# Last unit of the expert gather: eight late second halves and five homed rows instead of five and three

## The chip, the cores and the metric

One core of a Trainium2 chip runs the whole program. The metric is the device time of one execution in microseconds (us), lower is better; the figure for the kernel before is the median of three runs.

## What is computed

One decoder layer on 512 tokens of width 1024, all in float32: a mixing layer (stick-breaking attention beside a gated MLP), then an expert retrieval layer ("PEER"), then an input embedding gated by a sigmoid, with a layer norm after each. The change lies where the retrieval ends and the gate of the last 128 tokens begins:

```python
def block(args):                       # one tile of 128 tokens, 8 heads, 16 picks each
    xb, idb, gb = args
    ue = jnp.take(u_tab, idb, axis=0)
    h = jnp.einsum('thkd,td->thk', ue, xb)
    act = gb * jax.nn.gelu(h, approximate=False)
    ve = jnp.take(v_tab, idb, axis=0)
    return jnp.einsum('thk,thkd->td', act, ve)
...
x = layer_norm(ALPHA * x + ffn, ln2_g, ln2_b)
gate = jax.nn.sigmoid(x @ ple_wgate + ple_bgate)
x = layer_norm(ALPHA * x + gate * (p @ ple_wproj), ln3_g, ln3_b)
```

## The kernel before

The retrieval is cut into 32 units (NU), a unit being one head of one tile of 128 tokens; a unit has 16 picks (TOPK), which are called rows here. For each row GpSimd issues an indirect DMA (`gather_unit`, L658) that brings, for each of the 128 tokens, the 1024 numbers of the expert's u and, behind them in memory, the 1024 of its v: 8 KB to a partition, 1 MB in all. VectorE multiplies u by the token's x and sums it (`dots`, L1819), ScalarE takes the gelu and the gate and scales v by it (`activate`, L1435, L1438, L1445), and TensorE adds v, transposed in eight 128x128 blocks, to two banks of PSUM (`combine`, L1187). Consecutive units of one tile form a run; at a run's end VectorE adds its sum to the accumulator `acc` of the tile.

The rows lie in a ring of 13 parts of 1024 columns. A row takes two neighbouring parts, its u part being free again after five rows (U_LIFE) and its v part after eight (V_LIFE). So the issue of row n waits for the dots of row n-5 and for the combine of row n-8, both counted over all units. The issues stand in GpSimd's program in the order of the rows, and all of them go through one DMA queue.

The last unit, number 31, is treated differently:

- Rows from HOMED on (13, 14 and 15) go to buffers outside the ring, to `v_flat`, `wq_a` and `wq_r`, and wait only for the last query product, which was done long before.
- Rows from LATE on (11 to 15) are loaded without the last 512 columns of v ("late second halves"). Rows 14 and 15 are loaded as u alone at first, and the first half of their v follows in gathers of its own (L666).
- The late second halves come last on GpSimd, in gathers of 128x512 (L672, 0.25 MB each).
- For rows with a late half, ScalarE scales 512 columns instead of 1024, and `combine` does four block transposes instead of eight. The second halves are scaled and summed on VectorE into `late_sum` (`add_late`: L1889 for the first, L1892 for each further one), and their sum is turned into the PSUM bank by four transposes at once (L844).

Behind the last row VectorE's program has this order: scaling of row 15 (L2045), the addition of the upper PSUM half (`add_half`, L1880), of the lower one (`add_head`, L1873 and L1875), all `add_late`, then the upper half of y (L2055), its statistics (L1550 to L1561), a second `add_half` (L1880), centring and scaling (L1573, L2064, L1928), and the arguments of the gate (`gate_args`, L1918) that read TensorE's products. TensorE's program has the transposes of the accumulator (L844), the first half of the gate product of the columns 0 to 288, transposes, the first half of the columns 288 to 576, then a wait for the last `add_late`, the transposes of `late_sum`, two more first halves, and `second_half(0)` to `second_half(3)` (L1082, all in float32; each matmul leaves two records). SyncE waits for the last late gather before it stores the other three tiles' results.

The order around the change is written by hand, with semaphores; there is no planner.

Of the kernel before, what the change touches and what calls it, by code (L numbers as in the profile page):

```python
# [15 lines left out]
P = 128  # L16
D = 1024
S = 512
NT = S // P
# [5 lines left out]
PH, TOPK, NKEY = 8, 16, 128  # L25
# [16 lines left out]
HALF = D // 2  # L42
REST = S - P

LATE = TOPK - 5
HOMED = TOPK - 3
GV_RING = 5
# [137 lines left out]
def build(nc, a, out):  # L185
    ctx = ExitStack()
    with ctx:
# [76 lines left out]
        def row(u, c):  # L264

            if u == NU - 1 and c >= HOMED:
                return (v_flat, wq_a, wq_r)[c - HOMED]
            part = (FIRST_PART + U_LIFE * (u * TOPK + c)) % PARTS
            return ring[:, part * D:(part + 2) * D]

        late_sum = row(NU - 1, LATE)[:, PART:2 * D]
# [183 lines left out]
        picks_ready = sem("picks_ready")  # L455
        mean_spread = sem("mean_spread")
        bias_spread = sem("bias_spread")
        bias_kept = sem("bias_kept")
        gate_arg = sem("gate_arg")
        gain_in = sem("gain_in")  # L460
        ln2_in = sem("ln2_in")
        ln3_in = sem("ln3_in")
        proj_in = sem("proj_in")
        gain_spread = sem("gain_spread")
# [13 lines left out]
        def _(sp):  # L478
# [100 lines left out]
            for p in (piece_of(NT - 1, 5), piece_of(NT - 1, 6)):  # L579
                sp.wait_ge(piece_taken[p % 2], p // 2 + 1)  # L580
            sp.dma_start(b_gate[0:1, :], a["ple_bgate"][:, :]).then_inc(gain_in, 16)
            for i, name in enumerate(("ln2_g", "ln2_b")):
                sp.dma_start(gain_rows[i * KD:(i + 1) * KD, :], a[name][0, :].rearrange("(k n) -> k n", k=KD))\
                    .then_inc(gain_in, 16)
            for dst, src in ((w_gate, a["w_gate"][:, :, :]), (pT, a["pT"][:, :, :])):
                sp.dma_start(dst, src).then_inc(tail_in, 16)
            sp.wait_ge(q_done, Q_NO[17] + 1)
            for dst, name in ((ln2_g, "ln2_g"), (ln2_b, "ln2_b")):
                sp.dma_start(dst[0:1, :], a[name][:, :]).then_inc(ln2_in, 16)
            load_wq(23)  # L590
            sp.wait_ge(sums_done, 2)
            sp.wait_ge(q_done, Q_NO[29] + 1)
            for k in range(2):
                sp.dma_start(w_proj[k], a["w_proj"][:, k, :]).then_inc(proj_in, 16)
            load_wq(21)
            sp.wait_ge(q_done, Q_NO[30] + 1)
            sp.wait_ge(gate_done, 2)
            for dst, name in ((ln3_g, "ln3_g"), (ln3_b, "ln3_b")):
                sp.dma_start(dst[0:1, :], a[name][:, :]).then_inc(ln3_in, 16)
            load_wq(26)  # L600
# [9 lines left out]
        def _(pool):  # L610
# [25 lines left out]
            def gather_unit(u):  # L636
                if u:
                    pool.wait_ge(ids_ready, u + 3)
                for c in range(TOPK):
                    if u == 0 and c in (0, 1, TOPK // 2):  # L640
                        pool.wait_ge(ids_ready, (0, 1, TOPK // 2).index(c) + 1)
                    if u == 0 and c == 0:
                        pool.wait_ge(score_done, 1)
                    if u == 0 and c == 4:
                        pool.wait_ge(gv_halves, 1)
                    if u == 0 and c == 7:
                        pool.wait_ge(gv_halves, 2)
                    if u == NU - 1 and c >= HOMED:
                        pool.wait_ge(q_done, NU)
                    else:  # L650
                        if u * TOPK + c >= U_LIFE:
                            pool.wait_ge(dots_done, u * TOPK + c - U_LIFE + 1)
                        if u * TOPK + c >= V_LIFE:
                            pool.wait_ge(slot_free, u * TOPK + c - V_LIFE + 1)
                    n = PART if u == NU - 1 and c >= LATE else 2 * D
                    if u == NU - 1 and c >= TOPK - 2:
                        n = D
                    nc.gpsimd.indirect_dma_start(  # L658
                        out=row(u, c)[:, 0:n], out_offset=None, in_=a["uv"][:, :],
                        in_offset=bass.IndirectOffsetOnAxis(ap=ids[:, u % 4, c:c + 1], axis=0),  # L660
                    ).then_inc(rows_in[c % V_LIFE], 16)
# [15 lines left out]

        @block.tensor
        def _(pe):
# [355 lines left out]
            def spread_gain(n):  # L1035
                if n == 0:
                    pe.wait_ge(ln2_in, 16 * 2)
                    pe.wait_ge(cols_kept, 1)
                elif n == 4:
                    pe.wait_ge(ln3_in, 16 * 2)  # L1040
                    pe.wait_ge(gate_arg, 2)
                else:
                    pe.wait_ge(gain_kept, n)
                mm(ps[:, 6 if n < 4 else 4, :], neg_one[0:1, :], gains[n // 2][0:1, n % 2 * HALF:(n % 2 + 1) * HALF],
                   start=True, stop=True).then_inc(gain_spread, 1)

            def gain_columns():

                pe.wait_ge(gain_in, 16 * 3)
                nc.tensor.transpose(ps[:, 6, 0:2 * KD], gain_rows, ident[0:2 * KD, 0:2 * KD]).then_inc(cols_done, 1)  # L1050
# [36 lines left out]
            def spread_mean():  # L1087

                pe.wait_ge(sums_kept, 1)
                pe.wait_ge(picks_ready, 2)  # L1090
                for j in range(2):
                    k = mm(ps[:, 4 + j, :], picks[:, 0, :], sum_rows[:, j * HALF:(j + 1) * HALF], start=True, stop=True)
                k.then_inc(mean_spread, 1)

            def spread_bias(j):

                if j:
                    pe.wait_ge(bias_kept, 1)
                else:
                    pe.wait_ge(gain_kept, 4)  # L1100
                mm(ps[:, 6, :], picks[:, 1, :], sum_rows[:, j * HALF:(j + 1) * HALF], start=True, stop=True)\
                    .then_inc(bias_spread, 1)

            def embedding_product(i, j, bank):
                t = TAILS[i]
                if i == 0 and j == 0:
                    pe.wait_ge(proj_in, 16 * 2)
# [66 lines left out]
            def combine(u, c):  # L1174
# [9 lines left out]
                for k in range(KD // 2 if halved else KD):  # L1184
                    if very_last and k == 0:
                        pe.wait_ge(last_scaled, 1)
                    i = mm(ps[:, run_bank(r) + k // 4, (k % 4) * P:(k % 4 + 1) * P],  # L1187
                           row(u, c)[:, D + k * P:D + (k + 1) * P], ident[:, :], is_transpose=True,
                           start=(first and k % 4 == 0), stop=last or (u == NU - 1 and c == LATE - 1 and k >= 4),
# [68 lines left out]
        def _(act):  # L1258
# [143 lines left out]
            def keep_bias(j):  # L1402
                act.wait_ge(bias_spread, j + 1)
                fn(gate_bias[:, j * HALF:(j + 1) * HALF], ps[:, 6, :], ACT.Copy).then_inc(bias_kept, 1)
# [25 lines left out]
            def activate_rows(u, cols, n):  # L1430
# [9 lines left out]
                for c in range(cols.start, cols.stop):  # L1440
                    act.wait_ge(actv_ready, u * TOPK + c + 1)
                    if u == NU - 1 and c == TOPK - 2:
                        act.wait_ge(values_in[0], 16)
                    r = row(u, c)[:, D:PART if u == NU - 1 and c >= LATE else 2 * D]
                    fn(r, r, ACT.Copy, scale=actv[:, i, c:c + 1]).then_inc(scaled, 1)  # L1445
# [77 lines left out]
        def _(dve):  # L1523
# [287 lines left out]
            def dots(u, g):  # L1811
# [3 lines left out]
                for c in range(g * GRP, (g + 1) * GRP):  # L1815
                    r = row(u, c)[:, 0:D]
                    dve.wait_ge(rows_in[c % V_LIFE], u * (16 * TOPK // V_LIFE) + 16 * (c // V_LIFE + 1))
# [64 lines left out]
            def add_late(c):  # L1882

                r = row(NU - 1, c)[:, PART:2 * D]
                weight = actv[:, (NU - 1) % 4, c:c + 1]
# [22 lines left out]
            def scale_gate(k):  # L1908

                if k == 0:  # L1910
                    dve.wait_ge(mean_spread, 1)
                v.scalar_tensor_tensor(out=w_gate[:, k, :], in0=w_gate[:, k, :], scalar=gcols[:, k, 0:1], in1=pair(4),
# [130 lines left out]
            dve.wait_ge(values_in[1], 16)  # L2043
            r = row(NU - 1, c)[:, D:PART]
            v.tensor_scalar(r, r, gel[:, i, c:c + 1], gates[:, i, c:c + 1], ALU.mult, ALU.mult).then_inc(last_scaled, 1)  # L2045
# [84 lines left out]
```

## Time and profile before

| what | value |
|---|---|
| median of 3 runs | 1428.01 us (1427.73 to 1430.0) |
| the profiled execution, its own time | 1430.31 us |
| span in the trace of that execution | 1428.6 us |
| busy: TensorE, VectorE, ScalarE, GpSimd | 1132.4, 1078.3, 936.5, 562.6 us |
| data moved by DMA | 584.06 MB, mean 409 GB/s |

The trace is of one execution, and its times count from the start of the span. Busy times are shares of an average over very different stages; what the change is worth must be read in the last 60 us. PE is TensorE (PEld its weight loads), DVE is VectorE, ACT is ScalarE, POOL is GpSimd. In a timeline a row gives the start, the duration, the engine, the line and the operation, the number of merged instructions, and in brackets the idle time before and what ended it.

### The profile page before, as it was taken

The page shows a single profiled execution, that of the slowest core. Times are in us where ns is not written, and L with a number is a line of the kernel's source. Part 1 is how long each engine was busy: PE and PEld are TensorE (multiplying, and loading weights), DVE is VectorE, ACT ScalarE, POOL GpSimd, SP SyncE. Part 2 cuts the span into 40 slices and gives each one's busy share as a digit, 9 for nine tenths or more (in the row PEclk, how much of TensorE's full clock was granted, in tenths as well). Part 3 has the DMA queues.
Part 4 walks back from the last instruction along what each step waited for, and adds up shares of the span by engine and source line. Part 5 has one row for each costly group of instructions (what it writes and reads, how often), then busy time and mean ns, then how long its engine had stood idle before and what let it go on. Part 6 is the DMA issues. An engine that isn't in the chain of part 4 may idle for free.

```text
span 1428.6 us, 19360 instructions
## 1 busy us (share of the span) xinstructions
PE 1132.4 (79%) x6804; PEld 882.6 (62%) x6804; DVE 1078.3 (75%) x2602; ACT 936.5 (66%) x1613; POOL 562.6 (39%) x535
## 2 busy tenths in 40 slices
PE   9999999988689877796646988877658776776666
PEld 4567777666676666675645557755556565555555
DVE  1488777668778886688757668888887788878867
ACT  2245677679878888766636666567666766667563
POOL 1044344334544344445324334444334343434341
PEclk9999999999889989899778987888788888888778
DMA  9799999999999999999999999999999999999994
GB/s 356 277 387 423 419 426 394 425 423 426 414 426 404 426 422 424 426 426 421 427 428 426 425 426 409 416 408 426 427 427 404 425 427 426 428 426 427 426 425 148
DMA packets 89787, 584.06 MB, mean 409 GB/s; under 512 B 9709, under 2 KB 15253, under 8 KB 22490
## 3 DMA queue, kind: packets, MB, share of 16 engines
q0 software_dynamic: 74288, 536.90, 89.9%
q1 hardware_dynamic: 15402, 45.92, 8.2%
q8 instruction: 53, 0.87, 0.2%
q14 instruction: 44, 0.36, 0.1%
HBM read 580.69 MB, written 2.10 MB: 408 GB/s over the span
## 4 chain that ended last, share of the span: by engine, by line
DMA 47%; PE 22%; DVE 18%; issue 7%; ACT 4%; POOL 2%; POOLq 0%; DVEq 0%; ACTq 0%
DMA arena<-in_uv,ids 47%; DVE arena L1819 9%; PE ps L1187 6%; PE ps L1082 2%; PE ps L1006 2%; PE ps L872 2%; POOL arena L658 2%; ACT arena L1445 2%; PE ps L702 1%; PE ps L692 1%; PE ps L685 1%; ACT actv L1438 1%; PE ps L949 0%; PE ps L942 0%; PE ps L769 0%
## 5 line engine op out<-in xcount | busy, mean ns | idle before, releaser
L658 POOL DMA_INDIRECT arena<-in_uv,ids x512 | 549.1, 1073 | 802.9 <-DVE hid L1819 527.8
L1187 PE MATMUL ps<-ident,arena 128*128 128x128 f32 x4076 | 613.9, 310 | 278.2 <-ACT arena L1445 277.1
L1187 PEld LDWEIGHTS ps<-ident,arena 128*128 128x128 f32 x4076 | 535.3, 160 | 378.2 <-ACT arena L1445 336.8
L1819 DVE CUSTOM_DVE_ANT_1 arena<-arena 128x1024 f32<-128x1024 f32 x384 | 468.4, 1224 | 195.4 <-DMA arena<-in_uv,ids 192.2
L1445 ACT ACTIVATE arena<-arena,actv 128x1024 f32<-128x1024 f32 x511 | 554.2, 1131 | 0.2
L1435 ACT ACTIVATE gel<-hid 128x2 f32<-128x2 f32 (+1 forms) x257 | 52.1, 203 | 378.6 <-DVE hid L1819 378.1
L1819 DVE CUSTOM_DVE_ANT_0 arena<-arena 128x1024 f32<-128x1024 f32 x128 | 155.5, 1225 | 64.9 <-DMA arena<-in_uv,ids 63.8
L1438 ACT ACTIVATE actv<-gel,gates 128x1 f32<-128x1 f32 x511 | 122.9, 287 | 8.4
L872 PE MATMUL ps<-arena 128*128 128x128 f32 x992 | 120.1, 281 | 0.0
L872 PEld LDWEIGHTS ps<-arena 128*128 128x128 f32 x992 | 118.0, 198 | 0.0
L1006 PE MATMUL ps<-arena 128*128 128x384 f32 x192 | 65.9, 486 | 0.0
L1082 PE MATMUL ps<-arena 128*128 128x512 f32 (+2 forms) x160 | 60.9, 529 | 0.0
L1483 ACT ACT_TABLE_LOAD x45 | 57.7, 1283 | 0.8
L1491 ACT ACT_TABLE_LOAD x45 | 57.7, 1283 | 0.8
L1006 PEld LDWEIGHTS ps<-arena 128*128 128x128 f32 x192 | 34.6, 190 | 19.1
L837 PE MATMUL ps<-arena 128*128 128x512 f32 x96 | 43.4, 595 | 1.7 <-DVE arena L1857 1.3
L1082 PEld LDWEIGHTS ps<-arena 128*128 128x128 f32 x160 | 30.2, 203 | 21.5 <-issue 18.9
L1819 DVE DVE_READ_ACCUMULATOR2_ANT hid<- 128x1 f32 x512 | 42.1, 82 | 0.0
L692 PE MATMUL ps<-arena 128*128 128x512 f32 x64 | 29.1, 597 | 0.7 <-ACT arena L1345 0.7
L837 PEld LDWEIGHTS ps<-arena 128*128 128x128 f32 x96 | 17.4, 191 | 19.6 <-issue 17.2
L685 PE MATMUL ps<-arena 128*128 128x512 f32 x64 | 29.5, 605 | 0.0
L1688 DVE TENSOR_TENSOR cands<-cands,topf 128x512 f32<-128x512 f32 x31 | 21.4, 692 | 1.1
(268 smaller groups left out, 1004.8 us busy)
## 6 DMA issues: line engine op xcount, KB each, us to landing
arena<-in_wq SPq DMA_DIRECT2D x10, 1024.0 KB, 9.3
arena<-in_uv,ids POOLq DMA_INDIRECT x519, 10.4
arena<-in_w_out SPq DMA_DIRECT2D x2, 2048.0 KB, 12.3
arena<-in_w_gate SPq DMA_DIRECT2D x1, 4096.0 KB, 16.8
arena<-in_w_out SPq DMA_DIRECT2D x3, 1024.0 KB, 13.9
arena<-in_w_k SPq DMA_DIRECT2D x4, 512.0 KB, 7.6
arena<-in_w_q SPq DMA_DIRECT2D x2, 1024.0 KB, 10.1
arena<-in_w_v SPq DMA_DIRECT2D x2, 1024.0 KB, 10.2
```

The source lines that it names most:

```text
L658: nc.gpsimd.indirect_dma_start(out=row(u, c)[:, 0:n], out_offset=None, in_=a["uv"][:, :], in_offset=bass.IndirectOffsetOnAxis(ap=ids[:, u ...
L837: i = mm(ps[:, bank, :], src[:, c, :], w[:, c, j * HALF:(j + 1) * HALF], start=(c == 0), stop=(c == WB - 1))
L872: i = mm(ps[:, 7, half * P:(half + 1) * P], wq[b][k][:, half * P:(half + 1) * P], x1T[t][:, k, :], start=(k == 0), stop=(k == KD - 1))
L1006: i = mm(ps[:, piece_bank(p), 0:REST], w[:, b * D + k * P:b * D + (k + 1) * P], xT[:, k, :], start=(k == 0), stop=(k == KD - 1), skip_grou ...
L1082: m = mm(ps[:, bank, place:place + c1 - c0], acc[t][:, k * P:(k + 1) * P], w_gate[:, k, c0:c1], start=(k == 0 and place == 0), stop=(k == ...
L1187: i = mm(ps[:, run_bank(r) + k // 4, (k % 4) * P:(k % 4 + 1) * P], row(u, c)[:, D + k * P:D + (k + 1) * P], ident[:, :], is_transpose=True ...
L1435: fn(gel[:, i, cols], hid[:, i, cols], ACT.Gelu).then_inc(gel_ready, 1)
L1438: fn(actv[:, i, c:c + 1], gel[:, i, c:c + 1], ACT.Copy, scale=gates[:, i, c:c + 1])\
L1445: fn(r, r, ACT.Copy, scale=actv[:, i, c:c + 1]).then_inc(scaled, 1)
L1483: act.preload_act_table_set("natural_log_exp_and_others")
L1491: act.preload_act_table_set("gelu_and_others")
L1819: v.tensor_tensor_reduce(out=r, in0=r, in1=x1[t], scale=1.0, scalar=0.0, op0=ALU.mult, op1=ALU.add, accum_out=hid[:, i, c:c + 1]).then_inc ...
```

## The change

LATE goes from TOPK - 5 to TOPK - 8, so rows 8 to 15 have a late second half. HOMED goes from TOPK - 3 to TOPK - 5, so rows 11 to 15 lie outside the ring: in `subk`, `v_flat`, `wq_a` and `wq_r`, and row 15 in two pieces of 1024 columns, `acc[1]` and `acc[2]`. The homed rows get waits that the buffers and the semaphores need: for the last key scores, for the dots of row c-8, and for row 15 the transposes of the first three tiles. Six semaphores are merged into three, with the counts adapted. The replacements of `row(...)` by `u_part` and `v_part` in `dots`, `combine`, `activate_rows` and `add_late` do nothing but find row 15.

```diff
-LATE = TOPK - 5
-HOMED = TOPK - 3
+LATE = TOPK - 8
+HOMED = TOPK - 5
...
             if u == NU - 1 and c >= HOMED:
-                return (v_flat, wq_a, wq_r)[c - HOMED]
+                return (subk, v_flat, wq_a, wq_r)[c - HOMED]
...
+        def u_part(u, c):
+
+            return acc[1] if u * TOPK + c == NU * TOPK - 1 else row(u, c)[:, 0:D]
+
+        def v_part(u, c, c0, c1):
+
+            return acc[2][:, c0:c1] if u * TOPK + c == NU * TOPK - 1 else row(u, c)[:, D + c0:D + c1]
...
-        mean_spread = sem("mean_spread")
-        bias_spread = sem("bias_spread")
+        gate_spread = sem("gate_spread")
...
-        gain_in = sem("gain_in")
-        ln2_in = sem("ln2_in")
-        ln3_in = sem("ln3_in")
-        proj_in = sem("proj_in")
+        side_in = sem("side_in")
+        norm_in = sem("norm_in")
...
                     if u == NU - 1 and c >= HOMED:
+                        if c == HOMED:
+                            pool.wait_ge(score_done, NU)
                         pool.wait_ge(q_done, NU)
+                        if c >= V_LIFE:
+                            pool.wait_ge(dots_done, u * TOPK + c - V_LIFE + 1)
+                        if c == TOPK - 1:
+                            pool.wait_ge(y_tr, 2 * (NT - 1))
...
                     nc.gpsimd.indirect_dma_start(
-                        out=row(u, c)[:, 0:n], out_offset=None, in_=a["uv"][:, :],
+                        out=u_part(u, c) if n == D else row(u, c)[:, 0:n], out_offset=None, in_=a["uv"][:, :],
...
-                    out=row(NU - 1, c)[:, D:PART], out_offset=None, in_=a["uv"][:, :],
+                    out=v_part(NU - 1, c, 0, HALF), out_offset=None, in_=a["uv"][:, :],
...
-                    out=row(NU - 1, c)[:, PART:2 * D], out_offset=None, in_=a["uv"][:, :],
+                    out=v_part(NU - 1, c, HALF, D), out_offset=None, in_=a["uv"][:, :],
```

## Rows read from the trace of the kernel before

**Rows 1.** The page: span, and two lines of its 40 slices

```profile
span 1428.6 us, 19360 instructions
...
DMA  9799999999999999999999999999999999999994
GB/s 356 277 387 423 419 426 394 425 423 426 414 426 404 426 422 424 426 426 421 427 428 426 425 426 409 416 408 426 427 427 404 425 427 426 428 426 427 426 425 148
```

**Rows 2.** Timeline of VectorE: dots of rows 9 to 12 and 15

```profile
1388.62 1.23 DVE L1819 CUSTOM_DVE_ANT_1 arena<-arena 128x1024 f32<-128x1024 f32 x1 [1.25 <-DMA arena<-in_uv,ids]
...
1391.06 1.23 DVE L1819 CUSTOM_DVE_ANT_1 arena<-arena 128x1024 f32<-128x1024 f32 x1 [1.21 <-DMA arena<-in_uv,ids]
...
1392.90 1.22 DVE L1819 CUSTOM_DVE_ANT_1 arena<-arena 128x1024 f32<-128x1024 f32 x1 [0.61 <-DMA arena<-in_uv,ids]
...
1394.74 1.23 DVE L1819 CUSTOM_DVE_ANT_1 arena<-arena 128x1024 f32<-128x1024 f32 x1 [0.61 <-DMA arena<-in_uv,ids]
...
1399.10 1.23 DVE L1819 CUSTOM_DVE_ANT_1 arena<-arena 128x1024 f32<-128x1024 f32 x1
```

**Rows 3.** Timeline of GpSimd: rows 10, 12 and 13, first and last late half

```profile
1380.31 0.94 POOL L658 DMA_INDIRECT arena<-in_uv,ids  x1 [1.53 <-DVE hid L1819]
...
1385.20 0.94 POOL L658 DMA_INDIRECT arena<-in_uv,ids  x1 [1.50 <-DVE hid L1819]
1386.44 1.73 POOL L658 DMA_INDIRECT arena<-in_uv,ids  x1 [0.30 <-issue]
...
1393.47 1.48 POOL L672 DMA_INDIRECT arena<-in_uv,ids  x1 [0.30 <-issue]
...
1400.22 0.95 POOL L672 DMA_INDIRECT arena<-in_uv,ids  x1 [0.30 <-issue]
```

**Rows 4.** The late gathers by line: count, durations, and time from issue to landing

```profile
L672 POOL DMA_INDIRECT arena<-in_uv,ids x5: 942/1479/1574, 1393.5 to 1400.2; - x5
...
DMA to landing us min/median/max: 3.6/5.1/7.5
```

**Rows 5.** Timeline of VectorE from the late additions to the gate arguments

```profile
1403.17 0.48 DVE L1889 TENSOR_SCALAR arena<-arena,actv 128x512 f32<-128x512 f32 x1
...
1403.78 3.40 DVE L1892 SCALAR_TENSOR_TENSOR arena<-arena,actv 128x512 f32<-128x512 f32 x4
...
1407.29 0.69 DVE L2055 TENSOR_TENSOR arena<-ps,arena 128x512 f32<-128x512 f32 x1
...
1409.85 0.68 DVE L1880 TENSOR_TENSOR arena<-ps,arena 128x512 f32<-128x512 f32 x1
...
1412.61 1.28 DVE L1928 SCALAR_TENSOR_TENSOR arena<-arena,rstd 128x1024 f32<-128x1024 f32 x1
...
1414.09 0.52 DVE L1918 SCALAR_TENSOR_TENSOR arena<-ps,rstd,arena 128x288 f32<-128x288 f32 x1 [0.20 <-PE ps L1082]
...
1416.07 0.52 DVE L1918 SCALAR_TENSOR_TENSOR arena<-ps,rstd,arena 128x288 f32<-128x288 f32 x1 [1.47 <-PE ps L1082]
```

**Rows 6.** Timeline of TensorE around the transposes of the late sum

```profile
1403.10 3.09 PE L1082 MATMUL ps<-arena 128*128 128x288 f32 x8
...
1408.17 0.60 PEld L844 LDWEIGHTS ps<-ident,arena 128*128 128x128 f32 x4
1408.41 0.60 PE L844 MATMUL ps<-ident,arena 128*128 128x128 f32 x4
...
1408.85 5.13 PE L1082 MATMUL ps<-arena 128*128 128x288 f32 x24
```

**Rows 7.** Windows: length, busy by engine, granted clock, DMA share, GB/s

```profile
1398.40:1401.80 3.40, 1.67 (x11) 1.17 (x11) 3.09 (x6) 3.16 (x8) 2.15 (x3) 0.98 0.66 219
1401.80:1405.20 3.40, 3.40 (x13) 2.70 (x12) 2.64 (x6) 0.42 (x1) 0.00 (x0) 0.52 0.45 142
1405.20:1408.60 3.40, 3.40 (x19) 2.67 (x18) 3.00 (x5) 0.00 (x0) 0.00 (x0) 1.00 1.05 404
1408.60:1412.00 3.40, 3.40 (x21) 2.98 (x20) 3.26 (x9) 1.49 (x2) 0.00 (x0) 1.00 0.03 10
```

More of the change, by code:

```diff
@@ L580, in _ @@
                 sp.wait_ge(piece_taken[p % 2], p // 2 + 1)
-            sp.dma_start(b_gate[0:1, :], a["ple_bgate"][:, :]).then_inc(gain_in, 16)
+            sp.dma_start(b_gate[0:1, :], a["ple_bgate"][:, :]).then_inc(side_in, 16)
             for i, name in enumerate(("ln2_g", "ln2_b")):
                 sp.dma_start(gain_rows[i * KD:(i + 1) * KD, :], a[name][0, :].rearrange("(k n) -> k n", k=KD))\
-                    .then_inc(gain_in, 16)
+                    .then_inc(side_in, 16)
             for dst, src in ((w_gate, a["w_gate"][:, :, :]), (pT, a["pT"][:, :, :])):
@@ L588, in _ @@
             for dst, name in ((ln2_g, "ln2_g"), (ln2_b, "ln2_b")):
-                sp.dma_start(dst[0:1, :], a[name][:, :]).then_inc(ln2_in, 16)
+                sp.dma_start(dst[0:1, :], a[name][:, :]).then_inc(norm_in, 16)
             load_wq(23)
@@ L593, in _ @@
             for k in range(2):
-                sp.dma_start(w_proj[k], a["w_proj"][:, k, :]).then_inc(proj_in, 16)
+                sp.dma_start(w_proj[k], a["w_proj"][:, k, :]).then_inc(side_in, 16)
             load_wq(21)
@@ L598, in _ @@
             for dst, name in ((ln3_g, "ln3_g"), (ln3_b, "ln3_b")):
-                sp.dma_start(dst[0:1, :], a[name][:, :]).then_inc(ln3_in, 16)
+                sp.dma_start(dst[0:1, :], a[name][:, :]).then_inc(norm_in, 16)
             load_wq(26)
@@ L1036, in spread_gain @@
                 if n == 0:
-                    pe.wait_ge(ln2_in, 16 * 2)
+                    pe.wait_ge(norm_in, 16 * 2)
                     pe.wait_ge(cols_kept, 1)
                 elif n == 4:
-                    pe.wait_ge(ln3_in, 16 * 2)
+                    pe.wait_ge(norm_in, 16 * 4)
                     pe.wait_ge(gate_arg, 2)
@@ L1047, in gain_columns @@
             def gain_columns():
-                pe.wait_ge(gain_in, 16 * 3)
+                pe.wait_ge(side_in, 16 * 3)
                 nc.tensor.transpose(ps[:, 6, 0:2 * KD], gain_rows, ident[0:2 * KD, 0:2 * KD]).then_inc(cols_done, 1)
@@ L1092, in spread_mean @@
                     k = mm(ps[:, 4 + j, :], picks[:, 0, :], sum_rows[:, j * HALF:(j + 1) * HALF], start=True, stop=True)
-                k.then_inc(mean_spread, 1)
+                k.then_inc(gate_spread, 1)
             def spread_bias(j):
@@ L1101, in spread_bias @@
                 mm(ps[:, 6, :], picks[:, 1, :], sum_rows[:, j * HALF:(j + 1) * HALF], start=True, stop=True)\
-                    .then_inc(bias_spread, 1)
+                    .then_inc(gate_spread, 1)
             def embedding_product(i, j, bank):
@@ L1106, in embedding_product @@
                 if i == 0 and j == 0:
-                    pe.wait_ge(proj_in, 16 * 2)
+                    pe.wait_ge(side_in, 16 * 5)
                 for k in range(2):
@@ L1187, in combine @@
                     i = mm(ps[:, run_bank(r) + k // 4, (k % 4) * P:(k % 4 + 1) * P],
-                           row(u, c)[:, D + k * P:D + (k + 1) * P], ident[:, :], is_transpose=True,
+                           v_part(u, c, k * P, (k + 1) * P), ident[:, :], is_transpose=True,
                            start=(first and k % 4 == 0), stop=last or (u == NU - 1 and c == LATE - 1 and k >= 4),
@@ L1402, in keep_bias @@
             def keep_bias(j):
-                act.wait_ge(bias_spread, j + 1)
+                act.wait_ge(gate_spread, j + 2)
                 fn(gate_bias[:, j * HALF:(j + 1) * HALF], ps[:, 6, :], ACT.Copy).then_inc(bias_kept, 1)
@@ L1443, in activate_rows @@
                         act.wait_ge(values_in[0], 16)
-                    r = row(u, c)[:, D:PART if u == NU - 1 and c >= LATE else 2 * D]
+                    r = v_part(u, c, 0, HALF if u == NU - 1 and c >= LATE else D)
                     fn(r, r, ACT.Copy, scale=actv[:, i, c:c + 1]).then_inc(scaled, 1)
@@ L1815, in dots @@
                 for c in range(g * GRP, (g + 1) * GRP):
-                    r = row(u, c)[:, 0:D]
+                    r = u_part(u, c)
                     dve.wait_ge(rows_in[c % V_LIFE], u * (16 * TOPK // V_LIFE) + 16 * (c // V_LIFE + 1))
@@ L1882, in add_late @@
             def add_late(c):
-                r = row(NU - 1, c)[:, PART:2 * D]
+                r = v_part(NU - 1, c, HALF, D)
                 weight = actv[:, (NU - 1) % 4, c:c + 1]
@@ L1910, in scale_gate @@
                 if k == 0:
-                    dve.wait_ge(mean_spread, 1)
+                    dve.wait_ge(gate_spread, 1)
                 v.scalar_tensor_tensor(out=w_gate[:, k, :], in0=w_gate[:, k, :], scalar=gcols[:, k, 0:1], in1=pair(4),
@@ L2043, in _ @@
             dve.wait_ge(values_in[1], 16)
-            r = row(NU - 1, c)[:, D:PART]
+            r = v_part(NU - 1, c, 0, HALF)
             v.tensor_scalar(r, r, gel[:, i, c:c + 1], gates[:, i, c:c + 1], ALU.mult, ALU.mult).then_inc(last_scaled, 1)
```

## The prediction, written before the changed kernel was run

> **What bounds the kernel now.** I read the page first. The DMA line shows 9 in all slices but the second and the last, and the rate stands near 426 GB/s until the last slice, where it falls to 148 [rows 1]. So the gathers set the pace up to some 1395 us, and nothing in the change alters their bytes. What is open is the end: when the last row's dots can run, and what lies behind them.
>
> Next VectorE's timeline in the last unit. Its dots wait for the DMA: rows 9 and 10 come 2.44 us apart (1388.62 to 1391.06), which is 1 MB at 426 GB/s. Rows 11 and 12, the first without their last 512 columns, come 1.84 us apart (1392.90 to 1394.74) [rows 2]. Row 15, of which only u is loaded at that point, starts at 1399.10 with no idle time before it: the transfer of 0.5 MB and the dots of 1.23 us are about equally long there.
>
> Then the chain behind row 15. VectorE does five late additions: L1889 at 1403.17, then four L1892 in 3.40 us, 0.85 us each with the gaps, done at 1407.18 [rows 5]. TensorE reaches the transposes of the late sum at 1408.17 (its weight load) [rows 6], 0.99 us after they could have run. So here **TensorE is the later one, with 0.99 us of slack for VectorE**. From there TensorE runs without a pause to the product that the second L1918 waits for, 1.47 us long, at 1416.07 [rows 5]. Behind that VectorE works without a pause to the end of the kernel. Every shift of TensorE at 1408 is therefore a shift of the end.
>
> **The change part by part.**
>
> *Rows 8, 9 and 10 lose their last 512 columns (gain on the path).* Three rows become due 0.60 us earlier each (2.44 - 1.84) [rows 2]. Sum 1.8 us: row 15 starts at 1397.3 instead of 1399.1. VectorE's dots (1.31 us with their read-out) and the shorter scalings of ScalarE fit into 1.84 us, as they do for rows 11 to 13 now. The bounds are 0 (the transfers gain nothing) and 1.8; I take 1.8, since rows 11 and 12 show just this effect.
>
> *TensorE and ScalarE do less for these rows.* Twelve transposes fewer, and 3 x 512 columns fewer to scale. Neither is what row 15 waits for, so this is worth nothing; it is covered by the DMA's pace.
>
> *Three further additions on VectorE (cost on the path).* 3 x 0.85 = 2.55 us [rows 5]. They stand between the addition of the lower half and L2055, with nothing ahead of them that waits longer. The eight additions begin at 1403.17 - 1.84 = 1401.33 and end at 1401.33 + 0.61 + 7 x 0.85 = 1407.89, so **0.71 us later** than now (1407.18). Beside them TensorE's own work, 1.84 us earlier, would be at the transposes at 1406.3; now it waits there for VectorE, up to 1407.9. That is 0.2 us before the present 1408.17. The sum of this: -1.8 of head start, +1.6 given back as a new wait of TensorE, **-0.2 us**.
>
> *VectorE's part behind it.* L2055 to L1928 move by +0.71. The second L1880 then ends at 1411.24 (now 1410.53); the first second half of the gate product needs it, and TensorE gets there after 16 of its 24 records at 0.214 us (5.13 / 24) [rows 6], at about 1412.0. So there is 0.8 us of room. L1928 ends at 1414.6, the first L1918 at 1415.1, and TensorE delivers for the second at 1415.9 (1416.07 - 0.2). Again 0.8 us of room. Nothing is added to the sum.
>
> *Three further gathers on GpSimd, and the homes.* GpSimd has now ten gathers behind row 15 instead of seven. The last late half is issued at 1400.22 and lands 3.6 us later [rows 3, 4]. If GpSimd kept its present time for the first late half, 1393.47, the eighth would go out at 1400.22 + 3 x 1.25 = 1404.0, or at 1405.8 at the 1.87 us that the slow issues take (1.57 + 0.30) [rows 4], and land at 1407.6 to 1409.4. VectorE wants it at 1407.04. Here the homes matter: row 11 no longer waits for the dots of row 6, nor row 12 for those of row 7 (its issue at 1385.20 was released by them, idle 1.50 us [rows 3]). Row 11 can follow row 10 (1380.31) at once, and so on at 1.24 us: row 15 at some 1386.5, the first late half at some 1390.3, the eighth at 1399.0 to 1403.4, landed at 1402.6 to 1407.0. So the new waits on dots of rows 3 to 7 cost nothing (row 7's are done at 1384.9), and the gathers stay ahead of VectorE, though at the slow end by nothing at all. I take 0; the bounds are 0 and +1.2 (one more slow issue or a fuller queue). In the queue itself nothing overtakes: more gathers are waiting, and they land in the same order.
>
> *A page against the trace.* From issue to landing a late half takes 3.6 to 7.5 us [rows 4], yet one is issued every 1.25 to 1.87 us, so their fixed times lie beside each other. The Trainium skill's page "DMA: Bandwidth & Descriptors", section Bandwidth, asks for DMAs of at least 1 MiB, and its fit charges each DMA some 2.0 us beside its bytes. By that rule as a serial price three more gathers would add an estimated 6 us to the tail of transfers; the pace in the rows speaks against it, and the sum does not use it.
>
> *Merged semaphores, other waits.* The counts are passed in the same order as before, and the awaited events are over long before; score_done, q_done and y_tr are past at 1381. Cost 0. The stores of the three finished tiles start some 1 to 2 us later, behind the last late landing; they carry 1.5 MB and have 20 us until the last stores. Cost 0.
>
> **The sum.** -1.8 + 1.6 = -0.2 us on the profiled span of 1428.6. That execution took 1430.31 us, 1.7 us outside the span, and stands 2.3 us over the median; the difference of both kernels is what carries over. On the median of 1428.01 this gives 1427.8 us, with a range of its own of 1427.0 to 1428.6. About 0.2% (2.9 us) is what a measurement of this kernel can tell from no change, so this would read as no difference.
>
> **The rivals.**
>
> *Late halves come late, or the head start is smaller (1428.6 to 1429.7, middle 1429.0).* If the eighth late half lands at 1408.2, VectorE's sum and TensorE shift by +1.2, to +1.0 in all: 1429.0. The same if the rows gain only 0.6 of their 1.8 us. If they gain nothing, it is -0.2 + 1.8 = +1.6, 1429.6. For it: three of five late issues are slow, and the DMA moves just 219 GB/s from 1398.4 on [rows 7]. Against it: GpSimd gets 2 to 3 us ahead through the homes. Chance 0.23.
>
> *The head start arrives whole (1426.2).* VectorE's additions would have to be hidden, or to run closer than 0.85 us. An instruction takes 0.75 us, so seven could save 0.7 us, no more; the full -1.8 needs another cover that I don't see. Times of 1426.2 to 1427.0: chance 0.12.
>
> *Slower than before: the clock of TensorE.* The granted clock is 0.98 (of 2.4 GHz) at 1398.4 to 1401.8, where TensorE was busy 1.67 of 3.40 us, then 0.52, so essentially 1.2 GHz, until 1405.2, and 1.00 from there on, with TensorE busy throughout [rows 7]. The change puts a pause of some 1.6 us in front of the transposes. If the clock falls behind it, the 24 records of the product (and the next 8) take 0.386 us each (3.09 / 8, mostly at 0.52) instead of 0.214 [rows 6]: 32 x 0.172 = 5.5 us. All of it is on the path, 1433.3 us. It decides against the kernel once 18 of these records run slowly (3.1 us). Against it: TensorE works 5 us without a pause just before. Chance 0.07. The page "TensorE: Matmul & The Clock Gate" of the Trainium skill, in its part on the HAM clock gate, says that the clock falls to 1.2 GHz after idleness and rises after activity; by it the pause would have to count as idleness although TensorE works on both sides of it.
>
> *The change doesn't do what it says:* gathers of rows 8 to 10 are ahead of the dots as now, but come at the old pace because something else than bytes limits them. Then +1.6 as above; it is within the first rival. For other things unseen, on either side, 0.03.
>
> **How the numbers follow.** Forecast 1427.8 with 0.55, late halves 0.23, whole head start 0.12, clock 0.07, unseen 0.03. The range for 8 in 10 leaves out the clock and the unseen, and takes in the bounds of the first two rivals: 1426.2 to 1429.7. Faster by over 0.2% (under 1425.15) has no case of its own, only half of the unseen and the scatter of the whole head start: 0.04. Slower by over 0.2% (over 1430.87) is the clock, and scatter of the late halves: 0.10. Within 0.2%: 0.86.
>
> **What would show it.** Right: dots of rows 8 to 13 1.84 us apart, row 15's at 1.8 us earlier against the end of the span's gathers; seven L1892 at 0.85 us without a wait for the DMA; a wait of TensorE of 1 to 1.6 us for VectorE ahead of the L844 of the late sum; the first late half issued before 1392; the time from the second L1918 to the end unchanged. Wrong: L1892 waiting for a DMA (first rival); no wait of TensorE there (whole head start); a granted clock near 0.5 in the product behind the late sum (clock).

## The result, and the profile after

The changed kernel took **1432.3 us** (median of 19 runs, 1428.7 to 1440.6) against 1429.7 us for the kernel before (19 runs, 1426.7 to 1432.8), a ratio of **1.0018** with a 95% interval of 1.0009 to 1.0026. So it is slower by 2.6 us (1.3 to 3.7), where -0.2 was forecast, and it lies above the range.

The page shows the same bytes and the same DMA-bound body as [rows 1]; the last slice has become emptier (129 GB/s for 148). Lines of the page of after:

```profile
span 1432.4 us, 19348 instructions
...
GB/s 357 267 369 427 420 426 395 427 425 426 419 426 408 426 421 427 426 426 414 427 428 426 426 426 407 420 389 426 426 427 424 426 426 426 417 426 427 425 423 129
```

The spans of the two traces differ by 3.8 us, of which 2.16 are there when the last unit starts (its row 0 is issued at 1358.46, before at 1356.30). These are not the change's: 2.25 us are there at the very first gather (75.60 and 73.35 us), and the kernel before itself has that gather at 73.35 us in one trace and at 75.37 in another (e11). Over all the kernels below it starts anywhere from 72.9 to 75.6, and the order of the spans does not follow it. I therefore read only stretches inside the last 75 us.

VectorE in the last unit, timeline of after: the dots of rows 8, 9, 11, 12, 13 and 15, the late additions, L2066 and the two gate arguments. They answer to [rows 2] and [rows 5].

```profile
1387.69 1.23 DVE L1830 CUSTOM_DVE_ANT_1 arena<-arena 128x1024 f32<-128x1024 f32 x1 [0.62 <-DMA arena<-in_uv,ids]
...
1389.57 1.23 DVE L1830 CUSTOM_DVE_ANT_1 arena<-arena 128x1024 f32<-128x1024 f32 x1 [0.64 <-DMA arena<-in_uv,ids]
...
1393.25 1.22 DVE L1830 CUSTOM_DVE_ANT_1 arena<-arena 128x1024 f32<-128x1024 f32 x1 [0.61 <-DMA arena<-in_uv,ids]
...
1395.10 1.23 DVE L1830 CUSTOM_DVE_ANT_1 arena<-arena 128x1024 f32<-128x1024 f32 x1 [0.62 <-DMA arena<-in_uv,ids]
...
1396.97 1.23 DVE L1830 CUSTOM_DVE_ANT_1 arena<-arena 128x1024 f32<-128x1024 f32 x1 [0.64 <-DMA arena<-in_uv,ids]
...
1399.44 1.23 DVE L1830 CUSTOM_DVE_ANT_1 arena<-arena 128x1024 f32<-128x1024 f32 x1
...
1403.58 0.47 DVE L1900 TENSOR_SCALAR arena<-arena,actv 128x512 f32<-128x512 f32 x1
...
1404.19 5.17 DVE L1903 SCALAR_TENSOR_TENSOR arena<-arena,actv 128x512 f32<-128x512 f32 x6
...
1409.91 0.75 DVE L1903 SCALAR_TENSOR_TENSOR arena<-arena,actv 128x512 f32<-128x512 f32 x1 [0.56 <-DMA arena<-in_uv,ids]
...
1410.77 0.69 DVE L2066 TENSOR_TENSOR arena<-ps,arena 128x512 f32<-128x512 f32 x1
...
1417.97 0.52 DVE L1929 SCALAR_TENSOR_TENSOR arena<-ps,rstd,arena 128x288 f32<-128x288 f32 x1 [0.60 <-PE ps L1093]
...
1419.96 0.52 DVE L1929 SCALAR_TENSOR_TENSOR arena<-ps,rstd,arena 128x288 f32<-128x288 f32 x1 [1.46 <-PE ps L1093]
```

The head start is there: the dots of rows 8 to 13 are 1.84 to 1.88 us apart, and row 15's start 40.98 us after the unit's first issue (1399.44 - 1358.46) instead of 42.80. But the eighth addition waits 0.56 us for a DMA, and the additions take 7.08 us in all.

TensorE, timeline of after, answering to [rows 6]:

```profile
1405.53 0.60 PE L855 MATMUL ps<-ident,arena 128*128 128x128 f32 x4
1405.96 2.11 PE L1093 MATMUL ps<-arena 128*128 128x288 f32 x8
...
1410.72 1.12 PE L855 MATMUL ps<-ident,arena 128*128 128x128 f32 x4 [2.65 <-DVE arena L1903]
1411.63 6.24 PE L1093 MATMUL ps<-arena 128*128 128x288 f32 x24
```

TensorE pauses 2.65 us for VectorE, and what follows is slower than before: 1.12 us for the four transposes (0.60 before) and 6.24 us for the 24 records (5.13). The windows say why; in them the columns are as in [rows 7], the granted clock being third from the end:

```profile
1403.80:1407.20 3.40, 3.40 (x18) 2.69 (x17) 2.87 (x5) 0.00 (x0) 2.79 (x3) 1.00 0.71 184
1407.20:1410.60 3.40, 0.87 (x4) 0.36 (x2) 2.58 (x4) 0.00 (x0) 0.33 (x1) 0.98 0.37 128
1410.60:1414.00 3.40, 3.28 (x10) 2.65 (x11) 3.16 (x9) 0.60 (x2) 0.00 (x0) 0.52 0.98 377
1414.00:1417.40 3.40, 3.40 (x19) 2.93 (x18) 3.23 (x8) 0.89 (x1) 0.00 (x0) 1.00 0.23 89
```

Full clock until the pause, half clock (1.2 GHz) behind it just when the product on the path starts, full again later. The pause is 1 us longer than the 1.6 us of the prediction: 0.56 us of that is VectorE's wait for the DMA, and the rest is that TensorE, at its full clock here, comes to the transposes earlier than the prediction took from its one trace.

GpSimd, timeline of after, rows 14 and 15 (L669), the first halves of their v (L677), and the first and the last two late halves (L683); it answers to [rows 3]:

```profile
1388.22 1.51 POOL L669 DMA_INDIRECT arena<-in_uv,ids  x1 [0.30 <-issue]
1390.04 1.57 POOL L669 DMA_INDIRECT arena<-in_uv,ids  x1 [0.30 <-issue]
1391.91 1.55 POOL L677 DMA_INDIRECT arena<-in_uv,ids  x1 [0.30 <-issue]
1393.77 1.53 POOL L677 DMA_INDIRECT arena<-in_uv,ids  x1 [0.30 <-issue]
1395.60 1.54 POOL L683 DMA_INDIRECT arena<-in_uv,ids  x1 [0.30 <-issue]
...
1404.48 1.28 POOL L683 DMA_INDIRECT arena<-in_uv,ids  x1 [0.30 <-issue]
1406.07 1.47 POOL L683 DMA_INDIRECT arena<-in_uv,ids  x1 [0.30 <-issue]
```

From row 14 to the second late half the issues come some 1.85 us apart, not 1.24, and they end about 0.2 us after a landing: 1393.46, 1395.30 and 1397.14 stand behind the dots' starts at 1393.25, 1395.10 and 1396.97, which are released by the landings. So GpSimd goes at the pace of the rows here, as if the queue had no room for a further gather. The first late half leaves 37.14 us after the unit's first issue, as before (37.17), and the eighth at 1406.07 lands 3.8 us later, at 1409.9.

### The profile page after: what moved, and what is told of

Read it like the earlier page. It is cut to its first block, busy times and chain, and to the rows that moved or that the text cites. A ratio compares the mean times of both kernels' runs of the same rounds, so it can differ in the third digit from the quotient of the medians.

```text
span 1432.4 us, 19348 instructions
## 1 busy us (share of the span) xinstructions
PE 1128.4 (79%) x6792; PEld 879.9 (61%) x6792; DVE 1079.1 (75%) x2605; ACT 935.5 (65%) x1613; POOL 567.7 (40%) x538
## 4 chain that ended last, share of the span: by engine, by line
DMA 46%; PE 21%; DVE 17%; issue 7%; ACT 5%; POOL 3%; POOLq 0%; DVEq 0%
DMA arena<-in_uv,ids 46%; DVE arena L1830 9%; PE ps L1198 7%; ACT arena L1456 2%; PE ps L1017 2%; PE ps L703 2%; PE ps L883 2%; POOL arena L669 2%; PE ps L713 1%; PE ps L1093 1%; PE ps L696 1%; PE ps L848 1%; ACT actv L1449 1%; POOL arena L683 1%; PE ps L960 0%
## 5 line engine op out<-in xcount | busy, mean ns | idle before, releaser
L669 POOL DMA_INDIRECT arena<-in_uv,ids x512 | 549.8, 1074 | 801.0 <-DVE hid L1830 518.8
L1456 ACT ACTIVATE arena<-arena,actv 128x1024 f32<-128x1024 f32 (+1 forms) x511 | 552.9, 1129 | 0.2
L1093 PEld LDWEIGHTS ps<-arena 128*128 128x128 f32 x160 | 29.5, 199 | 20.6 <-issue 18.0
```

The lines of the kernel that those rows point to most:

```text
L669: nc.gpsimd.indirect_dma_start(out=u_part(u, c) if n == D else row(u, c)[:, 0:n], out_offset=None, in_=a["uv"][:, :], in_offset=bass.Indir ...
L1093: m = mm(ps[:, bank, place:place + c1 - c0], acc[t][:, k * P:(k + 1) * P], w_gate[:, k, c0:c1], start=(k == 0 and place == 0), stop=(k == ...
```

## The experiments

Each kernel below is derived from the changed one unless it says otherwise. "Tail" is the stretch from the start of row 15's dots to the end of the span, "behind" the part of it from the first late addition to the end. Times of the stretches are from one trace each, and the traces show effects that the timing is mostly too coarse to tell apart; ratios are to the kernel before, in runs on the same chip, with a 95% interval.

### e1: eight late halves, three homes

```diff
-HOMED = TOPK - 5
+HOMED = TOPK - 3
...
-                return (subk, v_flat, wq_a, wq_r)[c - HOMED]
+                return (v_flat, wq_a, wq_r)[c - HOMED]
```

> Eight late second halves, but three homed rows with the waits of the kernel before; merged semaphores as in the changed kernel. Theory A (the loss lies in the last 50 us: the eighth late half lands after VectorE wants it, and TensorE's pause ahead of the transposes of the late sum lets its clock fall): the first late half goes out at the same time whether three or five rows are homed, since the queue is full, so this kernel behaves like the changed one, +1.5 to +3 us on before, with one wait of VectorE for a DMA in its late additions and a pause of TensorE of 2 to 3 us. Theory B (the loss is upstream, from the homes, the merged semaphores or their waits): under +1 us.

Measured: 1.0027 (1.0016 to 1.0039), so +3.9 us, and 30.15 us behind. Theory A holds for the sign and the place, but the loss, the pause and the waits are larger than it said, and one sentence of it fell: the first late half goes out 38.98 us after the unit's first issue, not 37.1. So the two further homes are worth 1.8 us to GpSimd, and without them VectorE waits for the last two late halves, in the timeline of e1:

```profile
1407.03 0.75 DVE L1897 SCALAR_TENSOR_TENSOR arena<-arena,actv 128x512 f32<-128x512 f32 x1 [0.63 <-DMA arena<-in_uv,ids]
1408.76 0.75 DVE L1897 SCALAR_TENSOR_TENSOR arena<-arena,actv 128x512 f32<-128x512 f32 x1 [0.98 <-DMA arena<-in_uv,ids]
```

TensorE's pause is 3.83 us, and the 24 records behind it take 6.82 us.

### e2: homes and merged semaphores alone

```diff
-LATE = TOPK - 8
+LATE = TOPK - 5
```

> The changed kernel with five late second halves instead of eight: homes and merged semaphores alone. Theory A: as before within 0.5 us, the tail from the last row's dots to the end unchanged (29.5 us in the trace of before). Theory B: +1.5 to +2.6 us, all of it ahead of the last unit.

Measured: 1.0002 (0.9989 to 1.0015). The homes, their waits and the semaphores cost nothing that the timing or the trace shows, so theory B falls. The tail was not 29.5 us, though, but 27.86, 1.6 us **shorter** than in the first trace of the same order of work. TensorE had its full clock from row 15's combine to the end of the gate product, which led to e11.

### e3: first halves ahead of the wait

```diff
             first_half(1)
-            pe.wait_ge(late_added, TOPK - LATE)
-            transposes(run_bank(NR - 1) + 1, late_sum, 0).then_inc(last_summed, 1)
             first_half(2)
             first_half(3)
+            pe.wait_ge(late_added, TOPK - LATE)
+            transposes(run_bank(NR - 1) + 1, late_sum, 0).then_inc(last_summed, 1)
```

> The changed kernel, with TensorE's first halves of the last two column groups moved ahead of its wait for the late sum. Theory A: the pause of 2.65 us is filled with 3.4 us of work, the clock stays up; the product that the second L1929 waits for comes some 1.5 to 2 us earlier than in the changed kernel: 0 to +1 us on before. Theory B, or lateness of the gathers alone without the clock: no more than 0.6 us better than the changed kernel.

Measured: 1.0013 (1.0000 to 1.0025), some +1.9 us where 0 to +1 was expected, and 29.02 us behind: no gain in the trace. The first pause is filled, but a second opens behind it, since `second_half(0)` needs VectorE's L1891, and the clock falls there. TensorE in e3:

```profile
1405.38 5.13 PE L1093 MATMUL ps<-arena 128*128 128x288 f32 x24
1410.35 0.60 PE L855 MATMUL ps<-ident,arena 128*128 128x128 f32 x4
1412.95 3.31 PE L1093 MATMUL ps<-arena 128*128 128x288 f32 x8 [2.00 <-DVE arena L1891]
```

Eight records take 3.31 us there, which is 1.7 at the full clock. The pause comes from VectorE's lateness, and this order only moves it.

### e5 and e12: the pause filled with repeated work

```diff
             first_half(1)
+            first_half(1)
             pe.wait_ge(late_added, TOPK - LATE)
```

> The changed kernel, with the first half of the product for columns 288 to 576 computed twice, the second time over the first with the same result: 1.7 us of idle work that shortens the pause of 2.65 us to 0.9. Nothing else moves. Theory A with the clock as its larger part: the transposes of the late sum and the 24 records behind them run at a granted clock of 1.0 (0.60 and 5.1 us instead of 1.12 and 6.24), the end 1.0 to 1.6 us earlier than in the changed kernel. If the clock falls whatever TensorE does, or is not what costs: no difference to the changed kernel.

> The kernel with the repeated first half (pause filled) a second time, for its trace: if filling the pause is what holds the clock, the 24 records take 5.1 us again, and the stretch from the first late addition to the end is 27.4 us.

Measured: 27.42 and 27.44 us behind in the two traces, against 28.82 (and 29.03 in e9) of the changed kernel. The 24 records take 5.13 us in both. TensorE in e12:

```profile
1403.17 4.05 PE L1093 MATMUL ps<-arena 128*128 128x288 f32 x16
1408.08 0.66 PE L855 MATMUL ps<-ident,arena 128*128 128x128 f32 x4 [0.86 <-DVE arena L1904]
```

So in the traces the clock is 1.4 to 1.6 us of the loss, and work without use buys it back. The timing doesn't separate this from the changed kernel: 1.0016 (1.0002 to 1.0030) against 1.0018. The execution traced in e5 was also the fastest of its twelve (1429.07 us, with a median of 1431.78), so how often the filled pause keeps the clock is known from two executions only.

### e6: three gathers less

```diff
-            for c in range(LATE, TOPK):
+            for c in range(LATE + 3, TOPK):
                 nc.gpsimd.indirect_dma_start(
...
-                dve.wait_ge(late_in[c - LATE], 16)
+                if c >= LATE + 3:
+                    dve.wait_ge(late_in[c - LATE], 16)
```

> The changed kernel without the late gathers of rows 8, 9 and 10 (their second halves are not loaded; VectorE adds what lies there, so all eight additions stay). GpSimd then has seven gathers behind row 15, as before. Theory C (the late halves are priced by GpSimd's issues, 1.25 to 1.6 us each, not by their 0.6 us of transfer, and the last one comes late): the last late gather lands some 4 us earlier, VectorE's wait of 0.56 us for it disappears, TensorE's pause ahead of the late sum shrinks from 2.65 to about 2 us, and the stretch from the last row's dots to the end is 0.5 us shorter if the clock falls as in the changed kernel, 2 us shorter if it does not. If the gathers are not what delays, no wait is gone and the stretch stays at 33.0 us.

Measured: 1.0014 (0.9998 to 1.0030); tail 31.06, 26.92 us behind, as in the second case expected. VectorE no longer waits for a DMA, and its eight additions take 6.61 us. TensorE's pause is 1.27 us, and this time the clock holds (5.13 us for the 24 records). TensorE in e6:

```profile
1400.21 3.08 PE L1093 MATMUL ps<-arena 128*128 128x288 f32 x8
...
1406.94 0.66 PE L855 MATMUL ps<-ident,arena 128*128 128x128 f32 x4 [1.27 <-DVE arena L1904]
1407.43 5.13 PE L1093 MATMUL ps<-arena 128*128 128x288 f32 x24
```

The gathers are not the whole reason for the shorter pause. TensorE's first eight records took 3.08 us here and 2.18 in the trace of after, so TensorE came to the transposes 0.9 us later by its clock alone. With those records at the full clock the pause would have been an estimated 2.2 us, and no run shows whether the clock had held then. The timing doesn't separate this kernel from the changed one.

### e7: three additions less

```diff
-            for c in range(LATE + 1, TOPK):
+            for c in range(LATE + 1, TOPK - 3):
                 add_late(c)
```

> The changed kernel without the last three additions of late halves (rows 13 to 15 have no second half in the result; all eight gathers stay). Theory D (VectorE's additions are the cost): the additions end 2.6 us and the 0.56 us wait earlier, TensorE has no pause ahead of the late sum, its clock stays up, and the stretch from the last row's dots to the end falls from 33.0 us to 27.5 to 29, so the kernel is 0.5 to 2 us faster than before. If the loss lay in the gathers or upstream, it would stay near the changed kernel, 1 to 3 us slower than before.

Measured: 0.9989 (0.9974 to 1.0005), tail 28.49, 24.35 us behind. With all eight gathers, but five additions, the head start arrives: about -1.6 us, with an interval that just includes no change, but lies wholly below that of the changed kernel (1.0009 to 1.0026). The trace agrees: what lies behind the first addition is as long as in e11 and e2. This is the rival "head start whole" made real by leaving out its price.

### e8: six late halves

```diff
-LATE = TOPK - 8
+LATE = TOPK - 6
```

> Six late second halves instead of eight, five homed rows: one addition and one gather more than before, 0.6 us of head start. By the terms of the sum: TensorE has 0.99 us of slack, one addition takes 0.85 of it and the head start moves both, so there is no pause, no wait for a gather, and no reason for the clock to fall: the whole head start of 0.6 us should arrive, -0.6 us on before (0.9996). If each late half costs more than it gives from the first on, it is +0.5 us or more.

Measured: 0.9999 (0.9985 to 1.0012), 25.16 us behind, a pause of TensorE of 0.56 us. The expectation was wrong in its reason: there was no slack to take the addition. In the traces it has 0.8 us more behind the additions' start than e11, against 0.6 us of head start, which is nothing either way.

### e9 and e11: both kernels once more, for the trace

> The changed kernel a second time, for its trace. If TensorE's clock falls because of the pause ahead of the late sum (2.65 us in the first trace), it falls here too: transposes of the late sum and 24 records over 1.0 and 6.0 us, and the stretch from the first late addition to the end is 28.5 to 29 us. If the fall was chance, the stretch is 27.4 us as in the run with the pause filled.

> The kernel before a second time, for its trace. In its first trace TensorE ran at half clock for 3.4 us just as the gate product began, which made it 0.99 us late at the late sum; the run with homes alone had the full clock there and took 24.37 us from the first late addition to the end instead of 25.4. So this trace shows one or the other: 24.4 us with VectorE and TensorE about level at the late sum, or 25.4. The slack of 0.99 us on which the prediction stood is then a matter of the clock and not of the kernel.

Each is one execution. Measured: e9 has a pause of 2.04 us, the 24 records at 6.82 us and 29.03 us behind, so the clock fell in both traces of the changed kernel. It fell later in e9: the four transposes still took 0.65 us, not the 1.0 expected. e11 has 24.39 us behind instead of 25.43. VectorE and TensorE in e11:

```profile
1403.31 0.48 DVE L1889 TENSOR_SCALAR arena<-arena,actv 128x512 f32<-128x512 f32 x1
...
1405.16 0.60 PE L844 MATMUL ps<-ident,arena 128*128 128x128 f32 x4
1405.60 2.11 PE L1082 MATMUL ps<-arena 128*128 128x288 f32 x8
1407.38 0.52 PEld L844 LDWEIGHTS ps<-ident,arena 128*128 128x128 f32 x4
1407.54 0.60 PE L844 MATMUL ps<-ident,arena 128*128 128x128 f32 x4
```

The five additions take 4.02 us and end at 1407.33; TensorE loads the weights for the transposes of the late sum at 1407.38. The prediction compared 1407.18 and 1408.17 in [rows 5, 6]. **The slack of 0.99 us is not there** in this execution; it is 0.05 us. In the one trace that the prediction had it came from the half clock: the first eight records took 3.09 us (2.21 here), and the four transposes ahead of them 1.06 us (0.63 here).

### e10: ten additions, five late gathers

On top of e6, two further additions of the last row (ten in all):

```diff
             for c in range(LATE + 1, TOPK):
                 add_late(c)
+            for n in range(TOPK - LATE, TOPK - LATE + 2):
+                add_late(TOPK - 1, n)
```

> The kernel with three gathers less, and two additions more (ten in all; the last late half is added three times, so the result differs). The pause of TensorE grows from 1.27 us to 3.0 by VectorE's additions alone, with no gather late. Theory E (a pause of TensorE of over 2 us ahead of the late sum makes the clock fall behind it, whatever causes the pause): transposes and 24 records at about 1.1 and 6.2 us, the stretch from the first late addition to the end 26.9 + 1.7 + 1.4 = 30.0 us. If the additions cost only themselves: 28.6 us and a granted clock of 1.0.

Measured: 1.0040 (1.0026 to 1.0054), 31.42 us behind where 30.0 was expected, with a pause of 3.77 us instead of 3.0. TensorE in e10:

```profile
1411.02 1.12 PE L855 MATMUL ps<-ident,arena 128*128 128x128 f32 x4 [3.77 <-DVE arena L1905]
1411.93 7.46 PE L1093 MATMUL ps<-arena 128*128 128x288 f32 x24
```

Against e6 that is +4.50 us for two additions: 1.77 of them are the additions (8.38 - 6.61), the other 2.7 the clock, more than the 1.4 expected: 0.46 us in the transposes and 2.33 in the 24 records. By the ratios e10 is 3.7 us behind e6, with intervals that just overlap. So the clock falls behind a pause made by VectorE alone too. The price does not simply follow the pause: e10's of 3.77 us cost 2.7, but e1's of 3.83 us left the transposes at 0.66 us and the 24 records at 6.82, as e9's of 2.04 did. In windows of 1 us the granted clock is 0.50 from 1410 to 1416 in e10, and from 1411 to 1414 in e1.

### e13: six late halves, the first addition moved up

On top of e8:

```diff
+            add_late(LATE)
             dve.wait_ge(last_summed, 1)
             add_head(run_bank(NR - 1))
-            add_late(LATE)
```

> Six late halves and five homed rows, with the first late addition (0.48 us) moved ahead of the addition of the lower half, where VectorE waits 0.79 us for TensorE in the trace of six late halves. An attempt at a version that beats both kernels. Where that wait exists (TensorE at half clock in row 15's combine), some 0.5 us of the additions are hidden, and the stretch from the last row's dots to the end falls from 29.3 to 28.8 us; with the 0.6 us of head start that is 0.4 to 1 us better than before, too little to be told apart (0.9995). Where TensorE has its full clock there, VectorE has no idle time to fill and the lower half only comes later: no gain.

Measured: 1.0002 (0.9992 to 1.0012). In its trace TensorE had the full clock at row 15's combine and VectorE no idle time to fill, the case without gain. None of the versions that keep the whole result beats the kernel before.

## Why the prediction was wrong

The traces of all kernels together, with the pause of TensorE ahead of the late sum, the time of the 24 records behind it, and in the last column the stretch from the last unit's first issue to the end of the span, which holds the head start too:

| kernel | additions | late gathers | pause, us | 24 records, us | behind, us | last unit to end, us |
|---|---|---|---|---|---|---|
| before | 5 | 5 | 0 | 5.13 | 25.43 | 72.30 |
| e11 (before again) | 5 | 5 | 0 | 5.13 | 24.39 | 70.90 |
| e2 | 5 | 5 | 0 | 5.13 | 24.37 | 70.66 |
| e7 | 5 | 8 | 0 | 5.13 | 24.35 | 69.66 |
| e8 | 6 | 6 | 0.56 | 5.13 | 25.16 | 71.49 |
| e13 | 6 | 6 | 0 | 5.13 | 25.61 (one addition earlier) | 70.39 |
| e6 | 8 | 5 | 1.27 | 5.13 | 26.92 | 72.05 |
| e5, e12 | 8 | 8 | 0, 0.86 (filled) | 5.13 | 27.42, 27.44 | 72.25, 72.62 |
| after | 8 | 8 | 2.65 | 6.24 | 28.82 | 73.94 |
| e9 (after again) | 8 | 8 | 2.04 | 6.82 | 29.03 | 74.15 |
| e3 | 8 | 8 | 2.00, behind the 24 records | 5.13 | 29.02 | 74.20 |
| e1 | 8 | 8 | 3.83 | 6.82 | 30.15 | 75.33 |
| e10 | 10 | 5 | 3.77 | 7.46 | 31.42 | 76.55 |

Read as a sum from the 24.4 us at full clock: three additions +2.5 (e6), the late gather +0.5 (e5 against e6), the clock behind the pause +1.4 to +1.6 (after and e9 against e5). Together +4.4 to +4.6, less the 1.8 of head start: **+2.6 to +2.8 us**, where the timing gives +2.6 (1.3 to 3.7). How well this fits is in part luck. The sum takes the kernel before at full clock, and leaves out that its additions started 0.6 us sooner then (see the end of this section). By the last column the changed kernel is 1.6 us behind the first trace of before, 3.25 us behind the second when e9 is set against e11, and 2.4 us if the two traces of each are averaged. The terms come from one or two executions each.

Point by point:

- *Head start of three rows, -1.8.* Right: -1.82 in the trace, and it arrives at the end when the additions are left out (e7).
- *Three additions, +2.55.* The size was right (2.53). *The 0.99 us of slack that was to swallow part of it* is the step that failed first. I took "TensorE is the later one" from the one trace, although [rows 7] showed a clock of 0.52 over just the stretch that made it late. With the full clock the two engines are level (0.05 us apart in e11), and each addition costs itself in full (e8: +0.8). The trace of after had the full clock over most of that stretch (2.18 us for the first eight records), so there VectorE's lateness went straight to the path. Without the slack these two terms alone give -1.8 + 2.5 = +0.7 us, and not -0.2.
- *VectorE's part behind it has 0.8 us of room.* There was less: in e5, with TensorE at its full clock, VectorE does not wait for TensorE at the first gate argument, and waits 0.56 us at the second. It had no weight, since at the second argument TensorE's product came last in every trace.
- *Three gathers at 0.* Wrong by 0.5 us, inside the stated bounds of 0 to +1.2. The step that failed is "and so on at 1.24 us". Row 11 did follow row 10 at once (at 1383.70 after 1382.46), but from row 14 to the second late half each issue was held back until a landing, some 1.85 us apart, so the first late half left at the old time and not 3 us earlier. The working without homes (issue at 1404.0, landing at 1407.6) was nearly what happened in time from the unit's start (landing at 1409.9 - 2.16 = 1407.7). The homes did their part, 1.8 us (e1), and e2, in which five homes stand with five late halves, issues its first late half 34.8 us after the unit's first issue; the eight late halves used it up.
- *The serial price of 6 us for three gathers*, estimated from the fit on the Trainium skill's page "DMA: Bandwidth & Descriptors", did not come: the eight late gathers are issued 1.25 to 1.9 us apart and land 3.6 to 5.7 us after their issues, beside each other. But the time of the last one, 3.8 us from issue to landing for 0.25 MB, is on the path.
- *The clock, 7% and 5.5 us.* The mechanism was right; its size was too large, and its chance looks too low now that it came in both traces of the changed kernel. It took 1.4 to 1.6 us there, because the clock came back within the 24 records. I had set it low since TensorE works without a pause just before. The pauses that I can compare: 0.56, 0.86 and 1.27 us kept the clock, 2.00 (e3), 2.04, 2.65, 3.77 and 3.83 lost it. The "some 1.6 us" worked out lies between the two groups, where no run has a pause. The Trainium skill's page "TensorE: Matmul & The Clock Gate" says that the clock falls on idleness; these traces agree, and it stayed up in e5 and e12, where a repeated product fills the pause.
- *Late halves late, 23%*: this rival happened too, with a wait of 0.56 us. None of the rivals reaches +2.6 alone at its measured size; I had treated as alternatives what are links of one chain. The late gather and the missing slack lengthen the pause, and the pause lowers the clock.

What stays open: the start of the additions. It lies 3.5 us behind row 15's dots where TensorE had its full clock at row 15's combine (e2, e11), and about 4.1 where it had not. All nine traces with eight late halves have 3.85 to 4.2; those of five or six late halves have both (e13, whose first addition stands elsewhere, left out). It would fit that TensorE has less to do in those rows and so loses its clock more often, some 0.5 us more of cost, but no run isolates this. Nor is it settled what holds the issues back. In the kernel before an issue was held back with six gathers ahead of it (the first late half), in the changed one with five (row 14, 3.75 MB ahead). But in e2 the first half of row 15's v went out in 0.95 us with seven gathers and 4.5 MB ahead. So neither their number nor their bytes alone decide it.

## What to carry to other kernels

Slack read from one trace is only as good as the clock in it: before an engine's lateness is counted as room, look whether it ran at half clock in that very stretch, and redo the sum at the full clock. When an addition makes TensorE wait, price three things as one chain: the addition, the transfer it waits for, and the matmuls behind the pause at the lower clock. And moving small pieces of a transfer to the end trades DMA time (0.6 us a piece here) for issue time on GpSimd (1.25 us and more) and vector time (0.85 us); it pays only as long as another engine is in fact later.

## What the runs showed of the hardware

Pauses of TensorE of 0.56, 0.86 and 1.27 us ahead of or within the gate product left the granted clock at 1.00. Pauses of 2.00 us and more (2.00, 2.04, 2.65, 3.77, 3.83) were each followed by a stretch at 0.50, at a price of 1.4 to 2.7 us for the work behind it. In e1, e3 and e9 TensorE still worked about 1 us at the full clock before it fell. An issue of an indirect DMA on GpSimd takes 0.94 us, with 0.30 us to the next; where issues were held back they took up to 1.58 us and ended some 0.2 us after a landing, and one of 1.73 us stands in the traces without such a landing. An indirect gather of 128 x 2 KB with few others ahead of it lands 3.6 to 3.8 us after the start of its issue, against 0.6 us for its bytes at the full rate of 426 GB/s. The issue itself is in that time: 0.95 us of 3.6 in the kernel before, 1.47 of 3.8 in the changed one.
